# Norm gains multiplied into the turned x instead of into the weight units, in a five-mixer fp32 kernel on one core

## What is computed

```python
def rms_norm(x, g):
    y = xf * lax.rsqrt(jnp.mean(xf * xf, axis=-1, keepdims=True) + NORM_EPS)
    return (y * g).astype(x.dtype)
...
for i in range(DEPTH):                                   # DEPTH = 4
    m = mixer_i(rms_norm(x, norm_gains[i, 0]))           # h @ w_in, ..., o @ w_out
    x = x + rms_norm(m, norm_gains[i, 1])
    f = swiglu(rms_norm(x, norm_gains[i, 2]), ffn_w_gate[i], ffn_w_up[i], ffn_w_down[i])
    x = x + rms_norm(f, norm_gains[i, 3])
...
z = rms_norm_2(h, mix_norm) @ w_in
h = h + concatenate([attn, ssm]) @ w_out
gate = sigmoid(rms_norm_2(h, ple_norm) @ w_ple_gate)
h = h + gate * (p @ w_ple_proj)
```

## Time and profile before

| | us |
|---|---|
| median of 3 runs | 1369.65 |
| lowest and highest | 1369.13, 1371.83 |
| the profiled execution | 1370.82 |
| its span, first to last instruction | 1369.1 |
| PE busy | 1346.4 (98%) |
| DVE busy | 1020.4 (75%) |
| ACT busy | 790.7 (58%) |
| POOL busy | 177.1 (13%) |

### The profile page before, as it was taken

One profiled execution on the slowest core, in us unless ns is written; L12 is line 12 of the kernel. 1 busy time (PEld: TensorE's weight loads), 2 busy tenths in 40 slices (PEclk: granted clock), 3 DMA queues, 4 the chain that ended last, 5 costly groups with the idle time before them and its releaser, 6 DMA issues.

```text
span 1369.1 us, 20597 instructions
## 1 busy us (share of the span) xinstructions
PE 1346.4 (98%) x6811; PEld 1105.8 (81%) x6811; DVE 1020.4 (75%) x1930; ACT 790.7 (58%) x1546; POOL 177.1 (13%) x323
## 2 busy tenths in 40 slices
PE   7999999999999999999999999999999999999998
PEld 6888888889987888889888888888888888887657
DVE  6978666669666766669766665699887777889976
ACT  6676555456555655458656544566665455675344
POOL 4100000000111000002000000001049992000000
PEclk9999999999999999999999999999999999999999
DMA  8534766675433777783336777744457666553132
GB/s 283 165 124 132 237 215 222 215 242 188 158 106 113 241 215 222 231 244 109 123 106 210 222 231 229 231 165 158 126 178 229 227 216 214 171 184 123 62 123 93
DMA packets 180309, 249.24 MB, mean 182 GB/s; under 512 B 10392, under 2 KB 124640, under 8 KB 180240
## 3 DMA queue, kind: packets, MB, share of 16 engines
q1 hardware_dynamic: 152352, 224.05, 50.4%
q10 hardware_dynamic: 25920, 18.89, 4.6%
q0 software_dynamic: 1968, 5.43, 1.4%
HBM read 237.84 MB, written 10.49 MB: 181 GB/s over the span
## 4 chain that ended last, share of the span: by engine, by line
PE 83%; DVE 13%; ACT 3%; issue 1%; DMA 1%; ACTq 0%; SPq 0%; DVEq 0%
PE ps L2112 21%; PE ps L2114 21%; PE ps L2113 21%; DVE w_rest L1382 3%; PE ps L2118 3%; PE ps L2126 3%; PE ps L2122 3%; ACT w_head L830 1%; PE ps L2142 1%; PE ps L2448 1%; PE ps L2933 1%; PE ps L2934 1%; PE ps L2935 1%; PE ps L2965 1%; DVE x L1445 1%
## 5 line engine op out<-in xcount | busy, mean ns | idle before, releaser
L2112 PE MATMUL ps<-w_head,xt_head 128*128 128x512 f32 (+1 forms) x1152 | 448.0, 389 | 3.3 <-DVE w_rest L1382 2.9
L2114 PE MATMUL ps<-w_head,xt_rest 128*128 128x512 f32 (+1 forms) x1152 | 441.5, 383 | 0.0
L2113 PE MATMUL ps<-w_rest,xt_head 128*128 128x512 f32 (+1 forms) x1152 | 441.0, 383 | 0.0
L830 ACT ACTIVATE w_head<-w_raw,gain_t 128x512 fp32r<-128x512 f32 (+1 forms) x596 | 375.1, 699 | 84.2 <-PE ps L2114 24.1
L1382 DVE SCALAR_TENSOR_TENSOR w_rest<-w_raw,gain_t,w_head 128x512 fp32r<-128x512 f32 (+1 forms) x596 | 417.2, 764 | 5.5 <-ACT w_head L830 4.7
L2112 PEld LDWEIGHTS ps<-w_head,xt_head 128*128 128x128 f32 x1152 | 217.1, 188 | 48.3 <-issue 6.4
L2114 PEld LDWEIGHTS ps<-w_head,xt_rest 128*128 128x128 f32 x1152 | 217.1, 188 | 43.0
L2113 PEld LDWEIGHTS ps<-w_rest,xt_head 128*128 128x128 f32 x1152 | 217.4, 189 | 39.7
L830 ACT ACTIVATE w_head<-w_raw 128x1024 fp32r<-128x1024 f32 x124 | 124.6, 1053 | 81.6 <-PE ps L2114 76.9
L1380 DVE TENSOR_TENSOR w_rest<-w_raw,w_head 128x1024 fp32r<-128x1024 f32 x124 | 146.8, 1222 | 7.1 <-ACT w_head L830 6.7
L1990 DVE SCALAR_TENSOR_TENSOR hid<-ps,rstd_x,gate_s 128x256 f32<-128x256 f32 x88 | 38.5, 479 | 119.9 <-ACT gate_s L1126 119.9
(11 more groups left out here) (502 smaller groups left out, 1700.7 us busy)
## 6 DMA issues: line engine op xcount, KB each, us to landing
w_raw<-in_ffn_w_gate_dram SPq DMA_DIRECT2D x88, 512.0 KB, 4.3
w_raw<-in_ffn_w_up_dram SPq DMA_DIRECT2D x88, 512.0 KB, 5.9
w_raw<-in_ffn_w_down_dram SPq DMA_DIRECT2D x88, 512.0 KB, 6.2
w_raw<-in_a_w_in_dram SPq DMA_DIRECT2D x48, 512.0 KB, 4.8
w_raw<-in_b_w_in_dram SPq DMA_DIRECT2D x24, 512.0 KB, 4.7
w_raw<-in_w_in_dram SPq DMA_DIRECT2D x24, 512.0 KB, 4.6
hid_way<-q_t ACTq DMA_DIRECT2D x36, 256.0 KB, 2.0
k_t<-hid_way ACTq DMA_DIRECT2D x144, 64.0 KB, 5.1
```

The lines of the kernel that those rows point to most:

```text
L830: ins = act.activation(w_head[:, s, w], raw(u)[:, w], ACT.Copy, scale=1.0 if by is None else by)
L2112: pe.matmul(out_, hd, wh, start=first, stop=False)
L2113: pe.matmul(out_, hd, wr, start=False, stop=False)
L2114: return pe.matmul(out_, rt, wh, start=False, stop=last)
```

## The change

The gain no longer goes into the weights. ACT rounds each block of 128 columns of a turned group by itself, scaled by the column of `gain_t` that belongs to it, and DVE makes the rest of each block with the same factor: four steps a group on each engine where there was one. The semaphore goes up with the fourth. This is so at all ten entries (`in_columns` gives the four blocks; `ENTRY_ROWS` and the counter `entry` choose the gain).

All weight units are then rounded without a factor. `weight_units` now lists only how many steps a unit takes: four of 512 columns for the first three units of each mixer and of each feed-forward, and for the last four units; two of 1024 for all others, the window mixer's included. DVE's step becomes a plain subtraction of two operands. At the start ACT waits for `gain_t` ahead of groups 0 and 1, not behind them. PE's program, the loads and the order at the entries stay.

```diff
@@ -160,17 +160,12 @@
 def weight_units():
 
     out = []
-    for li, kind in enumerate(LAYERS):
-        out += [(4 * li, k, kt) for ch in in_chunks(kind) for _, _, k, kt in ch]
-        out += [(None, k, kt) for ch in out_chunks() for _, _, k, kt in ch]
-        gate_up = [(4 * li + 2, k, 4) for k in (0, 4)]
-        out += gate_up
-        for _ in range(NCH - 1):
-            out += gate_up + [(None, 0, 4)]
-        out += [(None, 0, 4)]
-    out += [(MIX_ROW, k, kt) for ch in col_units(3072) for _, _, k, kt in ch]
-    out += [(None, 0, 4)] * 6
-    return out + [(PLE_ROW, 0, 4), (PLE_ROW, 4, 4)] * 2
+    for kind in LAYERS:
+        out += [4] * 3 + [2] * (sum(len(ch) for ch in in_chunks(kind)) - 3)
+        out += [2] * sum(len(ch) for ch in out_chunks())
+        out += [4] * 3 + [2] * (3 * NCH - 3)
+    out += [4] * 3 + [2] * (L_UNITS - 3)
+    return out + [2] * 6 + [4] * 4
 
 
 def units_of(kind):
@@ -483,13 +478,17 @@
 
             return qkv[:, 0, 0:UNIT] if u == FIRST_GATE else w_raw[:, u % RING, :]
 
+        ENTRY_ROWS = [r for li in range(len(layer_names)) for r in (4 * li, 4 * li + 2)] + [MIX_ROW]
+
+        def in_columns(g, bank, row):
+
+            half, m = g % 2, g // 2
+            return [(4 * half + t, slice(P * m, P * m + P), ps[:, bank, P * t:P * t + P], gain_t[:, 4 * half + t, row:row + 1]) for t in range(4)]
+
         def pieces(u):
 
-            row, k0, kt = WEIGHTS[u]
-            if row is None:
-                return [(slice(1024 * h, 1024 * h + 1024), None, 2) for h in range(2)]
-            n = UNIT // kt
-            return [(slice(n * t, n * t + n), gain_t[:, k0 + t, row:row + 1], 1 if n == 512 else t % 2) for t in range(kt)]
+            n = UNIT // WEIGHTS[u]
+            return [(slice(i, i + n), n // 512) for i in range(0, UNIT, n)]
 
         def acc_bank(kind, m, c):
             return {"diff": 2 + 2 * m + c, "stick": 2 + m + 2 * c, "window": C_ACC[m, c]}[kind]
@@ -504,7 +503,7 @@
         def quarters_of(u, some):
 
             all_ = pieces(u)
-            return all_[some[0] * len(all_) // 4:some[1] * len(all_) // 4], sum(c for _, _, c in all_[:some[0] * len(all_) // 4])
+            return all_[some[0] * len(all_) // 4:some[1] * len(all_) // 4], sum(c for _, c in all_[:some[0] * len(all_) // 4])
 
         LAST_PARTS = ((0, 0, 0, 512, 3), (0, 1, 0, 512, 3), (1, 0, 0, 512, 1), (1, 1, 0, 256, 2), (1, 1, 256, 512, 5))
         LAST_HT = (xt_head[:, 6:8, :], xt_rest[:, 6:8, :])
@@ -824,19 +823,19 @@
                     act.wait_ge(unit_used, u - 3 * RING + 1)
                 elif u >= RING:
                     act.wait_ge(unit_used, u - RING + 1 + more * RING)
-                for i, (w, by, count) in enumerate(quarters_of(u, some)[0]):
+                for i, (w, count) in enumerate(quarters_of(u, some)[0]):
                     if between and i == 1:
                         between()
-                    ins = act.activation(w_head[:, s, w], raw(u)[:, w], ACT.Copy, scale=1.0 if by is None else by)
-                    if count:
-                        ins.then_inc(head_done, count)
+                    act.activation(w_head[:, s, w], raw(u)[:, w], ACT.Copy).then_inc(head_done, count)
 
             def entry(by_half, split=None, norm=True, groups=range(4), there=None):
 
                 for g in groups:
                     n["xt"] += 1
                     act.wait_ge(xt_ready, n["xt"])
-                    act.activation(group(xt_head, g, by_half), group_bank(g, by_half), ACT.Copy).then_inc(xt_head_done, 1)
+                    for k, w, src, by in in_columns(g, 6 + g % 2, ENTRY_ROWS[n["entry"]]):
+                        last = act.activation(xt_head[:, k, w], src, ACT.Copy, scale=by)
+                    last.then_inc(xt_head_done, 1)
                     if g == 1 and split is not None:
                         head(split)
                 if norm:
@@ -848,7 +847,9 @@
                 m, c = GATE_TURNS[i]
                 n["xt"] += 1
                 act.wait_ge(xt_ready, n["xt"])
-                act.activation(group(xt_head, 2 * m + c, True), group_bank(i, True), ACT.Copy).then_inc(xt_head_done, 1)
+                for k, w, src, by in in_columns(2 * m + c, 6 + i % 2, PLE_ROW):
+                    last = act.activation(xt_head[:, k, w], src, ACT.Copy, scale=by)
+                last.then_inc(xt_head_done, 1)
 
             def square_of_x(m, there=None):
                 if n["x"]:
@@ -950,6 +951,7 @@
             def close(kind, u, before_window=False):
 
                 these, banks = closing(kind, u)
+                n["entry"] += 1
                 squares_of(these[0:2])
                 if kind == "ffn":
                     head(u - 2 + RING, some=(0, 2))
@@ -1319,8 +1321,8 @@
                 act.wait_ge(lam_sum, 1)
                 act.activation(lam_e[:, :, :], lam_s[:, :, :], ACT.Exp).then_inc(lam_exp, 1)
 
+            act.wait_ge(gain_there, 1)
             entry(True, norm=False, groups=(0, 1))
-            act.wait_ge(gain_there, 1)
             head(0)
             head(1)
             rotary()
@@ -1372,30 +1374,26 @@
                     return
                 s = u % RING
                 these, there = quarters_of(u, some)
-                for w, by, count in these:
+                for w, count in these:
                     there += count
-                    dve.wait_ge(head_done, quarters(u) + there + (0 if count else 1) + more * 4 * RING)
-                    hd = w_head[:, s, w].bitcast(F32)
-                    if by is None:
-                        ins = dve.tensor_tensor(w_rest[:, s, w], w_raw[:, s, w], hd, ALU.subtract)
-                    else:
-                        ins = dve.scalar_tensor_tensor(w_rest[:, s, w], raw(u)[:, w], by, hd, ALU.mult, ALU.subtract)
-                    if count:
-                        ins.then_inc(rest_done, count)
-
-            def xt_rest_of(g, by_half):
+                    dve.wait_ge(head_done, quarters(u) + there + more * 4 * RING)
+                    dve.tensor_tensor(w_rest[:, s, w], raw(u)[:, w], w_head[:, s, w].bitcast(F32), ALU.subtract).then_inc(rest_done, count)
+
+            def x_rests(g, bank, row):
+
                 n["xt"] += 1
                 dve.wait_ge(xt_head_done, n["xt"])
-                dve.tensor_tensor(group(xt_rest, g, by_half), group_bank(g, by_half), group(xt_head, g, by_half).bitcast(F32),
-                                  ALU.subtract).then_inc(xt_rest_done, 1)
+                for k, w, src, by in in_columns(g, bank, row):
+                    last = dve.scalar_tensor_tensor(xt_rest[:, k, w], src, by, xt_head[:, k, w].bitcast(F32), ALU.mult, ALU.subtract)
+                last.then_inc(xt_rest_done, 1)
+
+            def xt_rest_of(g):
+                x_rests(g, 6 + g % 2, ENTRY_ROWS[n["entry"]])
 
             def gate_rest(i):
 
                 m, c = GATE_TURNS[i]
-                n["xt"] += 1
-                dve.wait_ge(xt_head_done, n["xt"])
-                dve.tensor_tensor(group(xt_rest, 2 * m + c, True), group_bank(i, True), group(xt_head, 2 * m + c, True).bitcast(F32),
-                                  ALU.subtract).then_inc(xt_rest_done, 1)
+                x_rests(2 * m + c, 6 + i % 2, PLE_ROW)
 
             def rsqrt(sums, width, count, rows=None):
 
@@ -1467,11 +1466,11 @@
                 dve.wait_ge(raw_done, n["add"] + 1)
                 entered(1, 1)
                 if before_window:
-                    xt_rest_of(2, True)
+                    xt_rest_of(2)
                 rest(u - 2 + RING, some=(1, 4))
                 if not before_window:
-                    xt_rest_of(2, True)
-                xt_rest_of(3, True)
+                    xt_rest_of(2)
+                xt_rest_of(3)
                 n["bank"] += banks
                 n["add"] += 1
                 n["sq"] += 4
...
```

More of the change, by code:

```diff
@@ L799, in _ @@
         def _(act):
-            n = dict(turn=0, xt=0, sq=0, bank=0, rstd=0, x=0, pair=0, o=0, oa=0, chain=0, ffn=0)
+            n = dict(turn=0, xt=0, sq=0, bank=0, rstd=0, x=0, pair=0, o=0, oa=0, chain=0, ffn=0, entry=0)
             scratch = []
@@ L1361, in _ @@
         def _(dve):
-            n = dict(chain=0, xt=0, sq=0, bank=0, add=0, rstd=0, pair=0, o=0, ffn=0, rope=0)
+            n = dict(chain=0, xt=0, sq=0, bank=0, add=0, rstd=0, pair=0, o=0, ffn=0, rope=0, entry=0)
             def step(ins):
@@ L1459, in residual @@
                 posted(part[1, 0], at[1, 0])
-                xt_rest_of(0, True)
-                xt_rest_of(1, True)
+                xt_rest_of(0)
+                xt_rest_of(1)
                 mean_begun(1, at[1, 0])
```

## The result

The changed kernel takes **1379.16 us** (median of 6 runs, 1377.45 to 1379.85), the kernel before 1369.52 beside it: ratio **1.0067**, 95% interval [1.0057, 1.0078]. It is 9.6 us slower; 1377 had been forecast, from 7.4 us lost. The profiled execution took 1379.64 us with a span of 1377.9 (before: 1370.82 and 1369.1).

The account below looks back on a forecast made before the run. PE was taken to bound the kernel, busy 98% of the span. Losses of 10.5 us at entries, start and gate, less 3.1 won where PE waits, gave +7.4 and a forecast of 1377 us, range 1368 to 1382.

Parts of the forecast that it names:

- What bounds: Whole kernel: PE busy 98% of the span; work taken off ACT and DVE pays only where PE waits.
- The price of a group: Turned x: four 128-column steps replace one, adding 0.56 us a group on ACT and 0.43 on DVE.
- The entries: Turns of new x: PE loses 6.2 us over six, 1.5 before the window mixer, 1.3 behind it.
- The 0.17 for the next head: At one entry, PE waits 0.17 us more for the head of group 2, after 0.86 lost at x(1,0).
- The start: First weights' rest ends at 12.1 instead of 11.3, 0.8 us lost; ACT's wait for gain_t costed at nothing.
- The gate: Gate part: the rest of group 0 ends 0.98 us later and PE's third turn loses 0.7.
- The last mixer: Nine wide units at 0.38 us each bring DVE ahead; gain 1.95 us, readout's wait gone, waits for p_t stay.
- The last feed-forward: Two waits of PE for ht_rest go, 0.5 us won.
- The diff layers: Two waits of PE for mix go, 0.7 us won.
- (a): Rival: the cover holds, entries lose only 0.2 us each; 0.3 us faster, 1369.4; chance 0.16.
- (b): Rival: last mixer gives all DVE saves, 3.4 us, and the clock stays up; 3.3 us faster, 1366.3; chance 0.09.
- (c): Rival: backlog spreads behind entries to the next weights' rest, 0.9 us more at each of eight; 1384; chance 0.13.

Follow-up runs that it names:

- x half: Changed kernel's four narrow x steps with vectors, but weight units rounded without a vector in as many steps as the kernel before: 1378.71 us, ratio 1.0065.
- weight half: Changed kernel's weight rounding kept, but x turned in one step per engine without vectors and gain_t's wait behind groups 0 and 1: 1366.23 us, 0.9969.
- change where it pays: Kernel before, with the change only for the last feed-forward and last mixer, one weight quarter moved later at three entries: 1366.71 us, ratio 0.9976.
- narrow mixer: Changed kernel with all the last mixer's weight units rounded in four steps without a vector: 1378.71 us, ratio 1.0071.
- quarter late: Changed kernel with one weight quarter on DVE moved behind the second norm at the mixer's entry: 1374.90 us, ratio 1.0041.
- ACT four: Changed kernel, ACT's four x steps kept, DVE's residual in one step without the vectors: 1373.28 us, ratio 1.0025.
- DVE four: Changed kernel, DVE's four x steps kept, ACT's head in one step without the vectors: 1372.66 us, ratio 1.0022.

## Why the prediction was right, and where it was off

- **What bounds.** Right: PE bounds, and work taken from ACT and DVE is worth something only in the last layers. 98 us less work brought 3.5.
- **The price of a group.** Right. ACT's four steps take 1.15 (said 1.16), DVE's 1.12 (said 1.12), from the nearest rows of the same form. By the table of the Trainium skill ("VectorE: DVE Perf Modes", the section on the TRN2 errata) such a step was an estimated 0.25 and 0.26; the rows show 0.38 and 0.34 for one record, but eight steps in 2.17 and 2.16, that is one every 0.26. The estimate fits the spacing. The advice against small tiles in the Trainium skill stands there for operands from SBUF; these steps read PSUM, DVE's the head from SBUF too, and here it holds in kind.
- **The entries.** Right in mechanism and size: 6.55 for 6.2, 1.76 for 1.5, 1.45 for 1.3. The one step that was mis-sized is DVE's end of the residuals, 4.11 where 3.98 stood, and with it the third turn, 0.99 later instead of 0.86. The 0.17 for the next head came as said. The runs add what the prediction had only implied: the delay is a chain over both engines, 0.82 from each alone and 1.26 from both.
- **The start.** The step that failed is "ACT's wait for gain_t ... I cost at nothing". The vectors were early indeed (whole at 4.80, x at 6.70), so nothing waited for them. What the prediction did not have is the table load: with the second wait in front it came behind the turned x, and cost 1.27. The other 0.68 is the 0.8 of the sum. PE's later instructions are 1.67 later and not 1.95, because its first products start 0.43 us apart, where later ones start 0.23 apart (the granted clock reads 1.00 in both), and this pace held longer in the kernel before: the last product at it starts 4.8 us behind the first there, 4.0 in the changed one. In the fourteen traces it is 2.3 to 4.8, and it differs between two executions of one kernel (4.8 and 4.0 before, 4.0 and 3.1 changed).
- **The gate.** Right: 0.83 for 0.7.
- **The last mixer.** The size is right (2.0 for 1.95, the waits for p_t stayed, the readout's wait went), the cause in part wrong: it was put down to wide steps, and 1.7 of 2.2 come from the missing vector. The size came out because the 0.38 a unit was read from rows that differ in both.
- **The last feed-forward** was under-sized, 1.13 for 0.5. The two waits for ht_rest had 0.47 of idle time, and each stood for 0.16 more between PE's instructions; some 0.3 of it I can't place. The saving a unit is larger there: DVE's step with the vector takes 1024 ns on average and not 741, a plain one 979 (x half alone), a wide one 1448, so a unit falls from 4.10 to 2.90, of which 0.18 is the vector and 1.02 the width. That fits the x half, which drops the vector alone and wins 0.07. POOL is busy 106 of 167 us in that stretch and not at all in the first feed-forward; that it makes DVE's steps longer is not tested.
- **The diff layers** were over-sized, 0.37 for 0.7: one of the two waits for mix is left, 0.3, though DVE has lighter weight steps ahead of it.
- **The rivals.** (a) fell with the rows of ACT and DVE, at their likely and not their lower bound. (b) wanted the clock to hold; it holds in some executions of either kernel, so it is no gain of the change; and the last mixer gave 2.2 up to the readout, not the 3.4 that DVE saves. (c): no wait of PE for w_rest stands behind any entry.

Of the 2.2 us between 1377 and 1379.2, 1.4 lie in the sum: 0.9 at the start, 0.9 spread over entries and gate, less 0.4 more won than said. The other 0.8 is how the profiled execution stands to the median: 0.5 above it, where 1.2 was taken over from the kernel before.

## What to carry to other kernels

A factor that differs by block can't ride along free where the whole tile was one step: it cuts the step into as many as there are factors, and that is dear exactly where the tile is on the way to the engine that bounds. Count first where the relieved engine is waited for; here two of nine places paid. The change at those two, with one weight quarter moved at three entries, won 0.24%, an estimated half of it by the moved quarter; the change everywhere lost 0.67%. And when a second wait is put ahead of ACT's first activation, look where the table load lands: a row of the timeline shows it.

## What the runs showed of the hardware

- ACT's table load (1.28 us) stands right before the first activation in the order of instructions. With one wait ahead of that activation in the program (kernel before, weight half, change where it pays) it ran at 0.82, while x landed later. With two waits (changed kernel, x half, narrow mixer, quarter late, ACT four, DVE four) the wait for the turned x was an instruction of its own in front of it, and it ran at 7.79 to 8.09. Asked for by name ahead of both waits, it ran at 0.82 again. The Trainium skill says the placement ("ScalarE: Activation LUTs", the step on the table-load gate: the compiler puts the load right before the activation that needs it), and the trace agrees; its 2.7 us with the drain is not seen here, where the heads begin 1.30 behind the load's start.
- A per-partition vector costs ACT 92 ns a step of 512 columns from PSUM (596 to 688) and DVE 60 (685 to 745). The Trainium skill gives 93 for a pointer operand of ACT ("ScalarE: Activation LUTs", "What ACT_TABLE_LOAD costs"), and the trace agrees.
- The same program, with the same wait of 0.95 us ahead, was granted half clock (1.2 GHz) for 3.4 us in one execution and full clock in the next. That is 1.7 us where it stands and 0.7 to 0.8 at the end of these two pairs of traces, so two single profiles are better compared by their instructions ahead of it than by their spans.
